# Prompt tile routed first in each layer, with half of its expert rows read beside the samples' delta rule and attention

## The reference, cut to what matters

```python
def trunk_layer(x, cvec, p, layer, ctx, rope):
    sh1, sc1, gt1, sh2, sc2, gt2 = modulation(cvec, p['w_mod'], p['b_mod'])
    h = rms_norm(x, p['g_norm1']) * (1 + sc1) + sh1
    mix, ctx_out = token_mixers(h, p, layer, ctx, rope)   # diff attention, latent attention, gated delta rule, then @ w_out
    x = x + gt1 * mix
    h = rms_norm(x, p['g_norm2']) * (1 + sc2) + sh2
    x = x + gt2 * peer_ffn(h, p['w_pq'], p['peer_keys'], p['peer_u'], p['peer_v'])
    return x, ctx_out

def peer_ffn(h, w_pq, peer_keys, peer_u, peer_v):
    q = (h @ w_pq).reshape(n, 8, 2, 128)
    sub = einsum('nhpd,hpkd->nhpk', q, peer_keys)          # 128 keys for each half
    sc, ix = top_k(sub, 16)                                # then top 16 of the 16 x 16 sums, softmax -> gates
    act = gelu(einsum('nd,nhkd->nhk', h, peer_u[experts])) # 8 heads x 16 experts for each token
    return einsum('nhk,nhkd->nd', gates * act, peer_v[experts])
```

## Time and profile before

| | us |
|---|---|
| median of 3 runs (lowest, highest) | 5211.7 (5206.11, 5214.82) |
| span of the profiled execution | 5217.8 |
| TensorE busy | 4403.5 (84%) |
| VectorE busy | 3444.6 (66%) |
| ScalarE busy | 1436.0 (28%) |
| GpSimd busy | 1498.3 (29%) |

### The profile page before, as it was taken

One profiled execution on the slowest core, in us unless ns is written; L12 is line 12 of the kernel. 1 busy time (PEld: TensorE's weight loads), 2 busy tenths in 40 slices (PEclk: granted clock), 3 DMA queues, 4 the chain that ended last, 5 costly groups with the idle time before them and its releaser, 6 DMA issues. The chain is left out here.

```text
span 5217.8 us, 51329 instructions
## 1 busy us (share of the span) xinstructions
PE 4403.5 (84%) x14836; PEld 2229.8 (43%) x14836; DVE 3444.6 (66%) x9196; ACT 1436.0 (28%) x4114; POOL 1498.3 (29%) x1410
## 2 busy tenths in 40 slices
PE   7999898888878878887788998988988788897776
PEld 3588665433323323322235886654333233332222
DVE  5555565667676777777565555746677767777775
ACT  2211342222222222222222113522222222222222
POOL 0122100333343434433301220004333334344432
PEclk9988899999999999999999888999999999999999
DMA  7100102899999999999870001019999999999997
GB/s 258 39 3 1 48 1 73 365 418 415 406 416 405 414 420 401 415 419 415 344 258 17 3 1 48 1 73 416 420 414 411 420 404 414 410 405 420 420 414 311
DMA packets 243939, 1481.06 MB, mean 284 GB/s; under 512 B 26384, under 2 KB 32144, under 8 KB 79296
## 3 DMA queue, kind: packets, MB, share of 16 engines
q0 software_dynamic: 184320, 1342.26, 62.5%
q1 hardware_dynamic: 59264, 135.37, 7.2%
q10 hardware_dynamic: 64, 0.07, 0.0%
HBM read 1473.96 MB, written 3.64 MB: 283 GB/s over the span
## 5 line engine op out<-in xcount | busy, mean ns | idle before, releaser
L1646 PE MATMUL psall<-left,diag 128*128 128x512 f32 x2848 | 1373.0, 613 | 323.3 <-ACT diag L1541 322.8
L1646 PE MATMUL psall<-right,diag 128*128 128x512 f32 x2272 | 1105.0, 617 | 265.7 <-ACT diag L1541 265.6
L1379 POOL DMA_INDIRECT left<-in_peer_uv,eidx x712 | 735.8, 1033 | 1797.3 <-PE psall L1646 1058.3
L1464 DVE CUSTOM_DVE_ANT_0 left<-left,mixed 128x1024 f32<-128x1024 f32 x712 | 873.2, 1226 | 543.1 <-DMA left<-in_peer_uv,eidx 543.1
L1646 PEld LDWEIGHTS psall<-left,diag 128*128 128x128 f32 x2848 | 500.1, 190 | 1163.8 <-ACT diag L1541 721.2
L1464 DVE CUSTOM_DVE_ANT_0 right<-right,mixed 128x1024 f32<-128x1024 f32 x568 | 696.8, 1227 | 422.3 <-DMA right<-in_peer_uv,eidx 422.3
L1548 ACT ACTIVATE act<-dot 128x1 f32<-128x1 f32 x1280 | 259.5, 203 | 2411.7 <-DVE dot L1464 2410.7
L1379 POOL DMA_INDIRECT right<-in_peer_uv,eidx x568 | 587.4, 1034 | 884.8 <-PE psall L1646 861.5
L1646 PEld LDWEIGHTS psall<-right,diag 128*128 128x128 f32 x2272 | 401.2, 191 | 945.3 <-ACT diag L1541 597.6
L1541 ACT ACTIVATE diag<-cons,wgt 128x128 f32<-128x128 f32 x1280 | 493.8, 386 | 2.3 <-issue 0.3
L498 POOL TENSOR_TENSOR mlt<-lt,lmask 128x512 f32<-128x512 f32 x120 | 173.0, 1452 | 535.6 <-DVE lt L596 370.8
(11 more groups left out here) (289 smaller groups left out, 5106.5 us busy)
## 6 DMA issues: line engine op xcount, KB each, us to landing
wlate<-in_w_mod SPq DMA_DIRECT2D x32, 1024.0 KB, 5.3
wq<-in_w_pq SPq DMA_DIRECT2D x64, 512.0 KB, 7.9
left<-in_peer_uv,eidx POOLq DMA_INDIRECT x712, 15.9
right<-in_peer_uv,eidx POOLq DMA_INDIRECT x568, 15.9
w<-in_w_mod SPq DMA_DIRECT2D x4, 2048.0 KB, 10.8
wtm<-in_w_mod SPq DMA_DIRECT2D x4, 2048.0 KB, 18.0
wtm<-in_w_in_tm SPq DMA_DIRECT2D x4, 2048.0 KB, 9.0
right<-in_w_out SPq DMA_DIRECT2D x4, 2048.0 KB, 11.4
```

The costliest lines, as they stand in the source:

```text
L1379: nc.gpsimd.indirect_dma_start(out=p.slots[n % SLOT], out_offset=None, in_=d["peer_uv"], in_offset=bass.IndirectOffsetOnAxis(ap=p.eidx[:, ...
L1464: nc.vector.tensor_tensor_reduce(out=u_row, in0=u_row, in1=p.mixed[:, t, :], scale=1.0, scalar=0.0, op0=ALU.mult, op1=ALU.add, accum_out=p ...
L1646: mm = nc.tensor.matmul(bank, p.diag[:, n % DIAGS, :], p.slots[n % SLOT][:, D + 512 * c:D + 512 * c + 512], start=(s == 0), stop=(s == UNI ...
```

## The change

The program of a layer is put into another order and split:

- `delta` is called twice. Part 0 has the head, the prompt's step 0, and all ten projection jobs (6, 7 and 8 in the head, 9 in step 0). It also stores the samples' `x` to DRAM (`mid_x`, 2 MB), so that its place in SBUF can be used.
- `prepare_attention` and `attend` are called for the prompt alone (16 short maps), with an own load of the latent weights and of `w_out`.
- `route_first` is new: output projection, residual, norm, 16 blocks of queries, scores and the top 16 of all 8 heads for tile 0, one head after another.
- `delta` part 1 (steps 1 to 4) and `attend` part 1 (64 long maps) carry D_ROWS = 64 of the 128 rows of tile 0: 8 in a step (one a level, two in levels 2 and 4), one in every two maps. GpSimd fetches them into D_SLOTS = 5 slots, VectorE takes the dot product, ScalarE does the gelu for two rows at once, the two gate products and the scaling of v (128x1024), and an accumulating DMA that GpSimd starts adds v to `p.acc`.
- `tail` starts its rows at once: first the other 64 rows of tile 0, then 512 of the samples (ROWS = 576). The prologue of tiles 1 to 4 is written between rows 0 and 24, for which only 5 slots are there, since the other 4 hold `w_out`; it is loaded again (4 MB), as is `x`. The rows of tile 0 are summed in pairs: v is multiplied by a 64-column diagonal for each half of the partitions, in four 64x64 blocks of the array a pair and half row, eight products where there were four. The `w_pq` blocks are now read once for each group as before, those of tile 0 in `route_first`.

The diff, cut to its core:

```diff
+    def fetch(self, e):
+        p = self.p
+        if e >= D_SLOTS:
+            self.summed(e - D_SLOTS + 1)
+        p.nc.gpsimd.indirect_dma_start(out=p.dslots[e % D_SLOTS], out_offset=None, in_=p.d["peer_uv"],
+                                       in_offset=bass.IndirectOffsetOnAxis(ap=p.eidx0[:, e:e + 1], axis=0)
+                                       ).then_inc(p.sem(f"first_in{e % D_SLOTS}"), 16)
+        if e >= 4:
+            self.add(e - 4)
+
+    def add(self, e):
+        p, pool = self.p, self.eng
+        pool.wait_ge(p.sem("first_scaled"), e + 1)
+        p.nc.gpsimd.dma_start(p.acc[:, :], p.dslots[e % D_SLOTS][:, D:2 * D], accum_op=ALU.add).then_inc(p.sem("first_sum"), 16)
...
+    def weigh(self, e):
+        if e < 0:
+            return
+        p, act = self.p, self.eng
+        if e % 2 == 0:
+            c = e % 8
+            act.wait_ge(p.sem("first_dots"), e + 2)
+            p.nc.scalar.activation(p.act0[:, c:c + 2], p.dot0[:, c:c + 2], ACT.Gelu_apprx_tanh).then_inc(p.sem("first_gelus"), 1)
+            act.wait_ge(p.sem("first_gelus"), e // 2 + 1)
+            for i in range(2):
+                p.nc.scalar.activation(p.wgt0[:, c + i:c + i + 1], p.act0[:, c + i:c + i + 1], ACT.Copy,
+                                       scale=p.gat0[:, e + i:e + i + 1]).then_inc(p.sem("first_weights"), 1)
+            act.wait_ge(p.sem("first_weights"), e + 2)
+        v_row = p.dslots[e % D_SLOTS][:, D:2 * D]
+        p.nc.scalar.activation(v_row, v_row, ACT.Copy, scale=p.wgt0[:, e % 8:e % 8 + 1]).then_inc(p.sem("first_scaled"), 1)
...
+def delta_rows(s, lvl):
+    e = DELTA_ROWS * (s - 1) + lvl + (lvl > 2) + (lvl > 4) - 1
+    return (e, e + 1) if lvl in (2, 4) else (e,)
...
# ScalarE, end of a level of delta part 1, and after every second map of attend part 1
+                    if rows is not None:
+                        for e in delta_rows(s, lvl):
+                            rows.weigh(e - 2)
# VectorE, end of a level (after turn_heads, turn_key) and of every second map
+                    if rows is not None:
+                        for e in delta_rows(s, lvl):
+                            rows.dot(e)
...
# tail, TensorE
+                if u == 0:
+                    if s % 2 == 1:
+                        continue
+                    pe.wait_ge(sem("diags"), n + 2)
+                    for c in range(2):
+                        for q in range(2):
+                            for h in range(2):
+                                a, b = 64 * h, 64 * ((h + q) % 2)
+                                mm = nc.tensor.matmul(half_sums(h)[b:b + 64, 512 * c:512 * c + 512], p.diag[a:a + 64, (n + q) % DIAGS, 0:64],
+                                                      p.slots[slot_of(n + q)][a:a + 64, D + 512 * c:D + 512 * c + 512],
+                                                      start=(s == 0), stop=(s == FIRST_ROWS - 2))
+                    mm.then_inc(sem("row_free"), 2)
+                    continue
```

More of the change, by code:

```diff
@@ L449, in _, with delta @@
                     last.then_inc(sem("conv_turned"), 1)
-def delta(p, lay):
+def delta(p, lay, part):
     nc, sem, ps = p.nc, p.sem, p.ps
@@ L582, in _, with dve_step @@
             dve.wait_ge(sem("egc"), 1)
-            for s in range(NT):
+        def dve_step(dve, own, s, rows):
+            if True:
                 for d in range(2):
@@ L652, in _, with pe_head @@
                                             ALU.add).then_inc(sem(f"step{d}"), 1)
[L654 to L659, removed]
+        @block.vector
+        def _(dve):
+            own = p.delta_chain = Chain(dve, sem("dve_delta")) if part == 0 else Chain(dve, p.delta_chain.sem, p.delta_chain.n)
+            if part == 0:
+                dve_head(dve, own)
+            else:
+                rows = DRows(p, lay, dve)
+            for s in tiles_of(part):
+                dve_step(dve, own, s, rows if part == 1 else None)
+        def pe_head(pe, project):
+            for j in range(CONV_JOBS, 6):
                 project(j)
@@ L938, in _ @@
                     nc.vector.tensor_copy(p.vb[:, t, :], b[:, :]).then_inc(sem("p_evd"), 1)
-            for t in range(1, NT):
+            for t in tiles if part == 1 else ():
                 copied(dve, at[("uq", t, 1)])
@@ L992, in _, with attend @@
                 last.then_inc(sem("p_mm"), 1)
-def attend(p, lay):
-    nc, d, sem, ps = p.nc, p.d, p.sem, p.ps
-    maps, outs = [], []
-    short, long = ([("b", 2 * g, "a", g, "b", 2 * g + 1, t) for t in tiles for g in range(HA)] for tiles in ((0,), range(1, NT)))
-    groups = []
-    for i, g in enumerate(long):
-        groups.append(g)
-        if i % (NT - 1) == NT - 2:
-            groups.append(short[i // (NT - 1)])
+def attend(p, lay, part):
+    nc, d, ps = p.nc, p.d, p.ps
+    sem = lambda name: p.sem(f"{name}_{part}")
+    tiles, nk = tiles_of(part), P if part == 0 else KEYS
+    first = tiles[0]
+    ts = slice(0, 1) if part == 0 else slice(1, NT)
+    maps, outs = [], []
+    groups = [("b", 2 * g, "a", g, "b", 2 * g + 1, t) for t in tiles for g in range(HA)]
     for *heads, t in groups:
@@ L1036, in attend, with _ @@
     with nc.Block() as block:
-        @block.sync
-        def _(sp):
-            for c in range(2):
-                sp.dma_start(p.wout[:, c, :, :], d["w_out"][bass.ds(lay, 1), :, :, WCH * c:WCH * c + WCH].rearrange("l p k n -> p (l k) n")
-                             ).then_inc(sem(f"load_wout{c}"), 16)
+        @block.gpsimd
+        def _(pool):
+            if part == 0:
+                return
+            rows = DRows(p, lay, pool)
+            for m in range(len(maps)):
+                for e in attend_rows(m):
+                    rows.fetch(e)
+            rows.last_sums()
         @block.tensor
@@ L1189, in _ @@
                     weigh(out_after[m][0])
+                if part == 1:
+                    for e in attend_rows(m):
+                        rows.dot(e)
             dve.wait_ge(sem("a_out"), len(outs))
-            for t in range(NT):
+            for i, t in enumerate(tiles):
                 x = p.mixed[:, t, 0:256]
-                if t >= 1:
-                    dve.wait_ge(sem("squares_a"), t)
+                if i >= 1:
+                    dve.wait_ge(sem("squares_a"), i)
                 own.link(nc.vector.tensor_tensor(p.junk[:, 0:256], x, x, ALU.mult))
@@ L1781, in layer @@
+                dring = sb(first, "dring", [P, 3, 2 * D], side="right")
+                flat = p.x[:, 1:NT, :].rearrange("p t n -> p (t n)")
+                p.dslots = [dring[:, i, :] for i in range(3)] + [flat[:, 2 * D * i:2 * D * i + 2 * D] for i in range(2)]
+                with ExitStack() as c3:
+                    delta_tiles(p, c3)
+                    p.delta_sems += p.names_of(delta, lay, 1)
+                    p.idle += [p.sem(name) for name in p.cleared]
             with ExitStack() as c2:
-                p.qTa = sb(c2, "qTa", [P, 2, TOK])
```

1044 lines of the change are left out of this document (642 added, 402 removed).

## The result

| | before | after |
|---|---|---|
| median (lowest to highest), us | 5213.3 (5206.1 to 5218.9) | 5732.6 (5732.4 to 5734.8) |
| span of the profiled execution | 5217.8 | 5730.6 |
| TensorE's mean granted clock | 0.963 | 0.872 |

The changed kernel takes 1.0999 times the time of before (95% interval 1.0982 to 1.1015). The forecast was 5300, with a range up to 5430: the direction was right, the size was not.

What follows compares the result with a forecast made beforehand. The row stream was taken as bound by DMA bytes, delta and attention by TensorE and hand-overs. Costs of 254 against a gain of 209 made +45 a layer, +90 in two: 5217.8 becomes 5308, less 6.1: 5300 us, range 5130 to 5430.

Steps and rivals of the forecast that it cites:

- projection jobs: Delta's head and steps: two more jobs in the head, three steps lose one, step 0 gains one; 9 us a layer.
- `route_first`: Prompt's routing before any row can be read: 29.5 us to the first MAX8, eight heads 77; 107 (100 to 120).
- split and block edges: Prompt and samples handled apart: latent projections 8 us, short maps filling and draining alone 5, four more block edges 5.
- rows in the steps: Delta stage: level 2 wait, dots, table load and a row 4.6 late; 14 us a step, 56 (23 to 100).
- rows in the maps, last sums: Attention: two rows per four maps stretch the groups, 60 us (8 to 222); four last sums overhang, 4 (0 to 20).
- gain of the tail: Tail moves fewer bytes and its DMA engines start at once: mean 1761 us becomes 1552, gain 209 a layer.
- loop of a slot: GpSimd's fetch waits for an earlier row's sum, which starts after the row ahead: 7.5 us (5.1 to 12.2).
- ScalarE's wait in level 2: Delta steps: `weigh` waits for a dot behind `turn_heads`, delaying `t1s`; 5.8 us a step, 23 as lower bound.
- The lower bound of 8 for the maps: Attention by busy time alone: ScalarE at 11.0 us against a group's 10.49 costs 0.5 a group, 16 cost 8.
- Slow sum: Sum costs as much as a row, loop 12.2 us: +215 a layer, 5730; chance 0.07.
- Products in series: Tail's 64x64 products run one after another, 6.9 us a pair: about +100 a layer, 5500; chance 0.08.
- Rows ride along: Sum doesn't queue behind the row, engines slip past one another: rows cost 41 us instead of 120, time 5144; chance 0.30.

Runs made afterwards that it cites:

- no rows in front: The changed kernel with `D_ROWS` 0: prompt still routed ahead and stages split, all 128 prompt rows read in the tail; 5454.6 us, 1.0446.
- the sum ahead: The changed kernel with GpSimd issuing the accumulating DMA of row e - 4 before the fetch of row e instead of behind it; 5439.6 us, 1.0429.
- small dots: The kernel with dots only, its dots taken over 8 of the 1024 columns; 5255.2 us.
- dots only: The changed kernel with `weigh` empty: rows in front fetched and dotted, without gelu, gate products, scaling or sum; 5333.1 us.
- VectorE's sums: The changed kernel with VectorE scaling v and adding it in one instruction, without DMA sums or ScalarE's scaling; 5415.7 us, 1.0391.
- VectorE with filling: The kernel in which VectorE scales and adds v, plus two 256-column TensorE products ahead of each map's scores; 5385.1 us, 1.0339.

## Why the prediction was wrong

Per layer, layer 0, us. The measured front is split by the kernel with no rows in front.

| step of the prediction | predicted | measured |
|---|---|---|
| projection jobs | 9 | 22: 119.6 - 99.4 in head and step 0, 282.0 - 280.0 in the steps |
| `route_first` | 107 | 117.5 |
| split and block edges | 18 | 14: 48.4 + 230.1 - 264.1 |
| rows in the steps | 56 | 135 |
| rows in the maps, last sums | 64 | 165 |
| gain of the tail | 209 | 195 |
| net | +45 | +259 |

**The step that failed is the loop of a slot.** The prediction said "If the sum starts when the row in front of it is through, it adds 0.5 MB or 1.3: loop 7.4, I take 7.5". It measured 10.1. The order was right: the sum does wait behind the row. Its size was not: the row of this stage lands 6.8 after its issue and not 6.1, the sum ends 0.99 + 8.3 - 6.8 = 2.5 behind it and not 1.3, and from its landing to the next fetch there is 0.8 for which I had nothing. In the maps 32 x (10.1 - 7.5) = 83 of the 101 us missed are this by the sum. By the runs it is less: the order turned round gives back 65, leaving the sums out 73. So the term was mis-sized, and had it been right, the forecast would still have been short: with the sum ahead the net is +113 a layer, not +45.

**In the steps I priced the loop as a late row, not as a late mask.** I had one row 4.6 late in front of w. But GpSimd also makes the masked matrices; with a wait for a DMA in its list, each `mlt` is as late as the last sum. That is 135 us; without the sums it is 46, and with the sum ahead 53. It is tempting to put the 46 down to 32 dots of 1.26 on VectorE, 40 in all, but the runs don't bear that out: dots of 8 columns still cost 32 in the steps (37 in layer 1), so whole dots make 18.6 of the 50.1 of the kernel with dots only (13.5 in layer 1). Of the 32, 22 are TensorE busy for longer at a lower granted clock (264.7 us at 0.77 against 243.0 at 0.84); what lowers it there no run separates.

**ScalarE's wait in level 2** was the reason for 23 us. Taking the dots first gave back 4.1 a step of the 5.8. But leaving ScalarE's whole work out changed the steps by nothing (449.7 against 445.7), so the wait isn't ScalarE's own. That reason falls. The order also moved VectorE's dots out from behind the rotary block, which may be what gave the 4.1, but how they arise is open, and with VectorE's sums in the list the same order lost 9.

**The lower bound of 8 for the maps was no bound.** It came from busy times at full clock. With dots and nothing else the maps cost 49. Where the clock stayed up, in layer 1 with small dots, fetched rows cost 5. I had no term for TensorE's clock, though the page shows it beside each window. And "followed, a group takes 13.1" was low as well: without sums a group takes 16.3, at a granted clock of 0.77.

**Front without rows.** The heads take 9.64 each, as forecast 9.6, and the first 10.9; what was short is the way to the first maximum, 38.9 instead of 29.5. The jobs that left steps 1 to 3 gave nothing back: the steps take 282.0 with no row in front and took 280.0. The clock there went from 0.88 to 0.84, which may be why; no run shows it apart.

**The tail** was 14 long; its first stretch was 30 long, and the rest 16 short. From the stretch up to row 24 (127 against 97) one reads where: VectorE's list stands at row 2 until the gain row has landed, 41 us after the start and not 32, and then pairs follow about every 9.1, a job of 7 and a pair of 1.95, with TensorE busy for 67.9 of the 70 us from 1340 to 1410.

**The rivals.** "Slow sum", given 0.07, has the right mechanism, a loop of a slot that is longer than 7.5, and almost the right time (5730), but the time is luck in part. Its loop of 12.2 was too high, which makes 214 us for the maps where 165 were measured; against that its steps were 15 too cheap, the rest of the front 20, and the tail's gain 14 too large. "Products in series" is refuted: 16 records of a pair of rows in 1.95 us.

```profile
1358.55 1.95 PE L1963 MATMUL psall<-ring,diag 64*64 64x512 f32 x16
```

"Rows ride along" was to decide at 75 a layer for the rows. No kernel here that does a row's whole work comes near it, and the cheapest with whole dots, which leaves out gelu and sums, has rows at 49.1 + 44.3 = 93. That isn't proof that it could not come true: rows that are fetched, with dots of 8 columns, cost 79 in layer 0 and 41 in layer 1, where the clock stayed up.

Why no version here beats before is read from the same numbers: without any row in front a layer is 121 longer, and 64 rows taken from the tail bring 164 at most, so they may cost 43 in front. The cheapest that computes everything, VectorE with filling, costs 48.0 + 78.5 = 126.5.

## What to carry to other kernels

When a DMA's landing frees a slot, write the loop out with the queue in it, and issue what frees the slot ahead of the large transfer; here two lines in the other order were worth 5% of the kernel. Ask of the engine that waits for it what else stands in its list: GpSimd's wait cost more through the masks behind it than through the rows. And price added work in a stage that is bound by TensorE at the clock that the profile grants it, not at the full one; here added work changed that clock, so read it again after the change, in each layer.

## What the runs showed of the hardware

- An accumulating DMA of 512 KB within SBUF, issued by GpSimd: 4.7 us from issue to landing ahead of a 1 MB row, 8.3 behind one, and 4.5 with no row near; a plain copy behind a row 6.7, with none near 2.9.
- TensorE at a granted clock of 0.75 for 100 us and more in which it is never idle in the trace: once in each group of 13.7 us it goes from 2.4 to 1.2 GHz for about 7 us. In the kernel with dots only it fell to 0.50 in the window from 866 to 876, behind one in which TensorE was busy for 5.4 of 10 us at the start of the maps, and the swing went on after the last row had landed. The same list with no row in front also falls at the start of the maps (0.61 from 806 to 816), then is at 1.00 for most of them, and so is layer 1 of the kernel with small dots, whose layer 0 swings. Two filling products a map brought it to 1.00, and the maps became 4 us longer for 58 us of added work. The Trainium skill (TensorE: Matmul & The Clock Gate, HAM oscillation) tells of such a swing for a TensorE that waits for data in each tile; here it goes on without a wait that the trace lists. What sets it off and what keeps it going I can't say: a wait too short for the trace, as records of matmuls have modelled ends, isn't excluded.
